# Two of four weight sums per column pair: from VectorE subtractions to transfers that add in SBUF

## The chip, the cores and the metric

The kernel runs on one core of one Trainium2 chip. The metric is device time of one execution in microseconds (us). Every instruction and transfer of one profiled execution is in the trace. PE is TensorE's matmul row, PEld its weight loads, DVE is VectorE, ACT is ScalarE, POOL is GpSimd, SP is SyncE, which only issues transfers. A PE product can wait for DVE, which can wait for ACT, which waits for transfers; the text speaks of such chains by these names.

## The reference

One layer of a streaming encoder for 512 prompt tokens and 32 sample tokens (544 together), width 1024. What matters here is the first large product, the input projection, whose columns then feed three branches:

```python
h = rmsnorm(x, g1)
z = h @ w_in
(mq, mk, mv, mo, mi, mf, sb, sc, sx, dq, dk, dv, gt) = jnp.split(z, splits, axis=-1)
...
proj = jnp.einsum('btnc,ncd->btnd', br, w_br)
gates = jax.nn.sigmoid(gt.reshape(Bsz, T, N_BRANCH, D_MODEL))
x = x + jnp.einsum('btnd,btnd->btd', gates, proj) @ w_o
h2 = rmsnorm(x, g2)
up = h2 @ w_up
...
x = x + (jax.nn.silu(upc[..., :D_FF]) * upc[..., D_FF:]) @ w_dn
```

The three branches are an mLSTM recurrence (`ml` steps), a short convolution, and differential attention (`at` steps); everything is float32.

## The kernel before, in words

**Products.** Float32 accuracy is made of three reduced-precision matmuls: weight and activation are each split into a high and a low part (`w_h`, `w_l`, `a_h`, `a_l`), and high times high, low times high and high times low are summed in PSUM. All weights stream from HBM. A weight goes through: a transfer by SP into one of four slots of `raw` (512 KB each, `NRAW`), a copy by ACT that rounds to `w_h` (L1033), a subtraction by DVE that leaves `w_l` (L1332), then the matmuls. The parts have five slots (`NSPLIT`). One slot holds a unit of four 128x128 weight tiles; DVE and ACT split a unit four units (`AHEAD`) before PE multiplies with it.

**Pairs.** Thirty groups of 256 columns of `w_in` are called pairs: ("mq", 0), ("mv", 0), ..., ("sx", 1), ..., ("gt2", 3). A pair's weight is a 2x2 block matrix: two halves of the 1024 rows by two blocks of 128 columns, B11, B12, B21, B22, each 128 partitions x 512 floats (256 KB). The activations are 2x2 too (row half by token half). Each pair is computed with seven block products instead of eight, numbered w = 1 to 7 and run by `strassen_product`, twelve matmuls of 272 columns each. Products 1, 2 and 3 take a block of weights straight from `raw` (B11, B21, B22); products 4 to 7 take sums T4 to T7 of blocks. DVE makes these in `make_t` into four places of the buffer `tw`: T7 = B22 - B12, T5 = B12 - B11, T6 = T7 + B11, T4 = B21 - T6. Where the two items of a pair lie in neighbouring slots of `raw` (29 of the 30 pairs, `both`), T7 and T5 are one instruction of 1024 floats a partition (L1352); else each sum is one of 512 (L1356). The left factors S1 to S4 are sums of activations, made once at the start.

**Order.** All engines walk one list, `ORDER`, of products, drains, `ml`, `at` and `post` steps; each engine takes its own steps from it, in order, and waits on semaphores. `T_MAKES` says at which unit DVE makes a sum: T6 and T4 two units before they are split (`u_of(q, 6) - AHEAD - 2`), T7 and T5 a unit earlier. SP loads a pair's two items ((q, 0) with B11 and B12, (q, 1) with B21 and B22) in the order of use; a slot of `raw` is loaded again when its last reader is through (`wait_item_read`). POOL takes small steps of the `ml` and `at` chains (L840 to L842, L889, L951, L952), output transfers, and the low parts L929 and L846.

After the pairs come the output projection, the up-projection with its convolution, and the down-projection, which the change does not touch.

Of the kernel before, what the change touches and what calls it, by code (L numbers as in the profile page):

```python
# [6 lines left out]
ALU = mybir.AluOpType  # L7
# [3 lines left out]
P = 128  # L11
DM = 1024
# [38 lines left out]
def streaming_encoder_step(nc, x_prompt, x_sample, cache_k, cache_v, state_C, state_n, state_m, state_conv,  # L51
# [306 lines left out]
    def u_of(pair, w):  # L358
        return first_unit[n_of(pair, w)]


    both = [q for q in pairs if ITEMS.index((q, 0)) % NRAW + 1 == ITEMS.index((q, 1)) % NRAW]
    for q in pairs:
        u6 = u_of(q, 6) - AHEAD
        for w, e in ((7, u6 - 3), (6, u6 - 2), (5, u6 - 3 if q in both else u_of(q, 5) - AHEAD - 2),
                     (4, u_of(q, 4) - AHEAD - 2)):
            T_MAKES.setdefault(e, []).append((q, w))
    assert min(T_MAKES) >= 0
    for e in sorted(T_MAKES):
        for x in T_MAKES[e]:  # L370
            t_no[x] = len(t_no)
    for q, q2 in zip(pairs, pairs[1:]):
        made = {x: e for e, xs in T_MAKES.items() for x in xs}
        for w in T_SLOT:
            assert made[(q2, w)] > u_of(q, w) - AHEAD, (q, w)
        assert t_no[(q2, 6)] > t_no[(q, 4)] > t_no[(q, 6)] > t_no[(q, 7)]

# [48 lines left out]
    with ctx:  # L426
# [155 lines left out]
        for nm in (  # L582
# [4 lines left out]

                "wh_ready wl_ready t_ready part_used "

# [85 lines left out]

        def scale_of(pair):
            return 64 ** -0.5 if pair[0] == "dq" else 1.0

# [21 lines left out]
        def t_view(pair, w):  # L700
            return tw[:, T_SLOT[w], :].rearrange("p (k f) -> p k f", k=KQ)

# [11 lines left out]
        def wait_item(eng, item):  # L714
            i = ITEMS.index(item)
            eng.wait_ge(raw_in[i % NRAW], 16 * (i // NRAW + 1))

        def wait_whole(eng, g):

            what, w = UNITS[g][0:2]  # L720
            if g == 0:
                eng.wait_ge(S["if_in"], 16)
            elif what not in pair_no:
                wait_item(eng, what)
            elif w in QUARTER:
                wait_item(eng, (what, QUARTER[w][0]))
            else:
                eng.wait_ge(S["t_ready"], t_no[(what, w)] + 1)

# [28 lines left out]
        def _(sp):  # L758
# [18 lines left out]
            for i, item in enumerate(ITEMS):  # L777
# [35 lines left out]
        def _(pool):  # L813
# [179 lines left out]
        def _(act):  # L993
# [56 lines left out]
            for kind, a, n in ORDER:  # L1050
# [87 lines left out]
                elif kind == "p" and a[1] in copied[a[0]]:  # L1138
# [14 lines left out]
                    if w == 1 and q == ("sc", 0):  # L1153
                        act.wait_ge(S["dense_done"], block_of[("pr", 0, KD - 1)] + 1)
                    sc.activation(dst_of(q, blk, half), chain_bank(q, w), ACT.Copy, scale=scale_of(q))\
                        .then_inc(S["act_drained"], 1)
# [154 lines left out]
        def _(dve):  # L1311
# [23 lines left out]
            def make_t(q, w):  # L1335

                i = pair_no[q]
                B11, B12, B21, B22 = (quarter(q, k, blk) for k in range(2) for blk in range(2))
                x, y, op = {7: (B22, B12, ALU.subtract), 6: (t_view(q, 7), B11, ALU.add), 5: (B12, B11, ALU.subtract),
                            4: (B21, t_view(q, 6), ALU.subtract)}[w]  # L1340
# [4 lines left out]
                if w in (6, 4):  # L1345
                    dve.wait_ge(S["t_ready"], t_no[(q, {6: 7, 4: 6}[w])] + 1)
                if q in both and w == 7:
                    if i:
                        dve.wait_ge(S["wl_ready"], u_of(pairs[i - 1], 5) + 1)
                    s0 = ITEMS.index((q, 0)) % NRAW  # L1350
                    b = raw[:, s0:s0 + 2, :].rearrange("p s (k f) -> p s k f", k=KQ)
                    v.tensor_tensor(tw[:, 0:3:2, :].rearrange("p s (k f) -> p s k f", k=KQ), b[:, :, :, P:2 * P],  # L1352
                                    raw[:, s0, :].rearrange("p (k s f) -> p s k f", k=KQ, s=2), ALU.subtract)\
                        .then_inc(S["t_ready"], 2)
                elif not (q in both and w == 5):
                    v.tensor_tensor(t_view(q, w), x, y, op).then_inc(S["t_ready"], 1)  # L1356

# [20 lines left out]
            for kind, a, n in ORDER:  # L1378
# [57 lines left out]
                elif kind == "left":  # L1436
                    F11, F21 = (f_x[:, 0:KQ, HALF * half:HALF * half + HALF] for half in range(2))
                    F12, F22 = (f_x[:, KQ:KD, HALF * half:HALF * half + HALF] for half in range(2))
                    if a[0] == 0:
                        dve.wait_ge(S["f_ready"], KD)  # L1440
                        sum_left(a_f[:, S1], F21, F22, ALU.add)
                        dve.wait_ge(S["s_ready"], 1)
                        sum_left(a_f[:, S2], a_f[:, S1], F11, ALU.subtract)
                        sum_left(a_f[:, S3], F11, F21, ALU.subtract)
                    elif a[0] == 1:
                        dve.wait_ge(S["s_ready"], 3)
                        dve.wait_ge(S["al_ready"], KD)
                        sum_left(F11, F12, a_f[:, S2], ALU.subtract)
# [679 lines left out]
```

## Time and profile before

| | |
|---|---|
| median of 3 runs | 993.11 us (991.67 to 993.19) |
| profiled execution, its own time | 993.04 us |
| span of its instructions | 991.2 us |
| PE busy | 971.5 us (98%) |
| DVE busy | 690.3 us (70%) |
| ACT busy | 472.4 us (48%) |
| POOL busy | 162.8 us (16%) |
| SP's transfer queue, share of 16 DMA engines | 28.2% |

The span runs from the first to the last instruction; 1.8 us of the execution lie outside it. The pairs occupy PE from about 49 us to 518 us. A matmul of 272 columns starts 0.126 us after the one before it, so a product of twelve takes 1.51 us; the trace shows each as some 0.29 us long, because they overlap.

### The profile page before, as it was taken

The page shows a single profiled execution, that of the slowest core. Times are in us where ns is not written, and L with a number is a line of the kernel's source. Part 1 is how long each engine was busy: PE and PEld are TensorE (multiplying, and loading weights), DVE is VectorE, ACT ScalarE, POOL GpSimd, SP SyncE. Part 2 cuts the span into 40 slices and gives each one's busy share as a digit, 9 for nine tenths or more (in the row PEclk, how much of TensorE's full clock was granted, in tenths as well). Part 3 has the DMA queues.
Part 4 walks back from the last instruction along what each step waited for, and adds up shares of the span by engine and source line. Part 5 has one row for each costly group of instructions (what it writes and reads, how often), then busy time and mean ns, then how long its engine had stood idle before and what let it go on. Part 6 is the DMA issues. An engine that isn't in the chain of part 4 may idle for free.

```text
span 991.2 us, 20106 instructions
## 1 busy us (share of the span) xinstructions
PE 971.5 (98%) x7749; PEld 949.6 (96%) x7749; DVE 690.3 (70%) x1161; ACT 472.4 (48%) x982; POOL 162.8 (16%) x346
## 2 busy tenths in 40 slices
PE   7999999999999999999999999999999999999996
PEld 6999899998999998999999999999999999999996
DVE  7887666688666899877775547777777777634354
ACT  5675455565565766555553333333333333322242
POOL 2000121110111222021112211111111111111011
PEclk9999999999999999999999999999999999999999
DMA  6522323264321223233244212222222222432252
GB/s 198 197 86 86 93 92 108 68 197 136 104 85 45 86 86 86 64 89 105 66 134 168 86 61 92 85 97 91 89 86 87 85 86 81 128 94 76 84 148 94
DMA packets 104086, 99.87 MB, mean 101 GB/s; under 512 B 4868, under 2 KB 99481, under 8 KB 103735
## 3 DMA queue, kind: packets, MB, share of 16 engines
q1 hardware_dynamic: 98799, 85.51, 28.2%
q10 hardware_dynamic: 4072, 10.23, 3.0%
q0 software_dynamic: 1120, 2.86, 0.8%
q8 instruction: 62, 1.02, 0.4%
q14 instruction: 33, 0.27, 0.1%
HBM read 91.26 MB, written 7.31 MB: 99 GB/s over the span
## 4 chain that ended last, share of the span: by engine, by line
PE 90%; DVE 4%; issue 2%; ACT 2%; DMA 0%; POOL 0%; DVEq 0%; POOLq 0%; ACTq 0%
PE D L1751 51%; PE D L1810 28%; PE D L1770 2%; PE X L2045 1%; PE X L2083 1%; DVE w_l L1332 1%; ACT w_h L1033 1%; PE D L1782 1%; PE D L1937 1%; PE D L1895 1%; PE X L1991 1%; PE X L1992 0%; PE X L1977 0%; DVE tw L1352 0%; PE X L1994 0%
## 5 line engine op out<-in xcount | busy, mean ns | idle before, releaser
L1332 DVE TENSOR_TENSOR w_l<-raw,w_h 128x512 fp32r<-128x512 f32 (+1 forms) x286 | 201.0, 720 | 131.2 <-ACT w_h L1033 128.9
L1810 PE MATMUL D<-a_h,w_h 128*128 128x272 f32 x840 | 250.4, 298 | 1.4 <-DVE tmp L1513 1.0
L1810 PE MATMUL D<-a_h,w_l 128*128 128x272 f32 x840 | 243.6, 290 | 0.0
L1810 PE MATMUL D<-a_l,w_h 128*128 128x272 f32 x840 | 242.3, 288 | 0.0
L1033 ACT ACTIVATE w_h<-raw 128x512 fp32r<-128x512 f32 (+1 forms) x286 | 171.5, 617 | 82.8 <-PE D L1751 71.7
L1810 PEld LDWEIGHTS D<-a_h,w_h 128*128 128x128 f32 x840 | 158.7, 189 | 5.6 <-issue 2.6
L1810 PEld LDWEIGHTS D<-a_l,w_h 128*128 128x128 f32 x840 | 159.1, 189 | 0.0
L1810 PEld LDWEIGHTS D<-a_h,w_l 128*128 128x128 f32 x840 | 158.6, 189 | 0.0
L1751 PE MATMUL D<-h_h,w_h 128*128 128x272 f32 x704 | 145.9, 288 | 0.1
L1751 PE MATMUL D<-h_h,w_l 128*128 128x272 f32 x704 | 145.7, 288 | 0.0
L1751 PE MATMUL D<-h_l,w_h 128*128 128x272 f32 x704 | 145.1, 288 | 0.0
L1332 DVE TENSOR_TENSOR w_l<-tw,w_h 128x512 fp32r<-128x512 f32 x120 | 83.7, 704 | 39.6 <-ACT w_h L1033 33.6
L1751 PEld LDWEIGHTS D<-h_h,w_h 128*128 128x128 f32 x704 | 110.6, 188 | 0.3 <-DVE ups L1703 0.3
L1292 ACT ACTIVATE acc<-ups,fcw 128x546 f32<-128x546 f32 x44 | 33.1, 753 | 162.7 <-POOL ffn_last L975 162.7
L1751 PEld LDWEIGHTS D<-h_l,w_h 128*128 128x128 f32 x704 | 110.6, 188 | 0.0
L1751 PEld LDWEIGHTS D<-h_h,w_l 128*128 128x128 f32 x704 | 109.9, 189 | 0.0
L1033 ACT ACTIVATE w_h<-tw 128x512 fp32r<-128x512 f32 x120 | 75.2, 631 | 42.5 <-PE D L1751 15.0
L1751 PE MATMUL D<-g_h,w_h 128*128 128x272 f32 x352 | 80.6, 290 | 0.0
L1751 PE MATMUL D<-g_l,w_h 128*128 128x272 f32 x352 | 79.8, 288 | 0.0
L1751 PE MATMUL D<-g_h,w_l 128*128 128x272 f32 x352 | 79.8, 288 | 0.0
L1706 DVE SCALAR_TENSOR_TENSOR acc<-ups,fcw,acc 128x546 f32<-128x546 f32 x44 | 34.7, 789 | 57.9 <-ACT acc L1292 57.9
L1751 PEld LDWEIGHTS D<-g_h,w_h 128*128 128x128 f32 x352 | 57.9, 188 | 0.3 <-DVE xT L1682 0.2
(359 smaller groups left out, 1670.2 us busy)
## 6 DMA issues: line engine op xcount, KB each, us to landing
raw<-in_w_in SPq DMA_DIRECT2D x64, 512.0 KB, 4.2
raw<-in_w_up SPq DMA_DIRECT2D x44, 512.0 KB, 4.1
raw<-in_w_down SPq DMA_DIRECT2D x20, 512.0 KB, 3.8
raw<-in_w_branch SPq DMA_DIRECT2D x12, 512.0 KB, 3.4
raw<-in_w_out SPq DMA_DIRECT2D x8, 512.0 KB, 4.4
raw<-in_w_down SPq DMA_DIRECT2D x10, 384.0 KB, 3.5
x_spill<-xT ACTq DMA_DIRECT2D x1, 2176.0 KB, 7.4
xT<-x_spill ACTq DMA_DIRECT2D x1, 2176.0 KB, 10.3
```

The source lines that it names most:

```text
L1033: sc.activation(split_view(w_h, g), whole_view(g), ACT.Copy).then_inc(S["wh_ready"], 1)
L1292: sc.activation(acc[part][:, j % 2, 0:T + 2], ups[m % 2][:, 2:T + 4], ACT.Copy, scale=fcw[:, 2, jj:jj + 1])\
L1332: v.tensor_tensor(split_view(w_l, g), whole_view(g), split_view(w_h, g).bitcast(F32), ALU.subtract)\
L1706: link(v.scalar_tensor_tensor(out=ac, in0=u[:, 1:T + 3], scalar=fcw[:, 1, jj:jj + 1], in1=ac, op0=ALU.mult, op1=ALU.add))
L1751: last = t.matmul(banks(n)[:, half if at_bank is None else at_bank, 0:HALF], w[:, k, :], x[:, kx + k, HALF * half:HALF * half + HALF], sta ...
L1770: last = t.matmul(banks(n)[0:w.shape[2], half, 0:HALF], w[:, k, :], left_of(x, kx)[:, half, :], start=kx == 0 and i == 0, stop=kx == KD - ...
L1782: last = t.matmul(banks(n)[0:w.shape[2], half, 0:HALF], w[:, k, :], left_of(x, kx)[:, half, :], start=kx == 0 and i == 0, stop=kx == KD - ...
L1810: last = t.matmul(out, wt[:, k, :], x[:, left, k, :], start=w in (1, 2, 5) and k == i == 0, stop=k == KQ - 1 and i == 2, skip_group_check= ...
L1895: last = t.transpose(B[:, j // 4, P * (j % 4):P * (j % 4) + L], src[:, P * j:P * j + P], ident[0:L, 0:L])
L1937: last = t.transpose(B[:, P * c:P * c + P], src_tok(name, j)[:, P * c:P * c + P], ident[:])
L1991: t.matmul(o, qi[:, h, 0:L], C[:, h, :], start=True, stop=False)
L2045: t.matmul(X[:, c, 0:nk], dqT[d, h, P * i:P * i + P], dkT[d, h, 0:nk], start=True, stop=False, skip_group_check=True)
```

## The change

T5 and T7 are no longer made by DVE. For each pair:

- T7 = B12 + B22 is formed in place: POOL issues a transfer (`accum_op=add`) that reads B22 from HBM again and adds it to B12 where that lies in `raw`. Product 7 then takes its weight from `raw`.
- T5 = B11 + B12: SP loads B11 a second time, into place 0 or 2 of `tw` (alternating from pair to pair), and POOL issues a second adding transfer that brings B12.
- POOL issues both at a place of `ORDER` six units before the pair's first product (`SUMS_AT`), after waiting for the loads that they add to.
- DVE still makes T6 = T7 + B11 and T4 = B21 + T6, and now waits for the T7 transfer before T6; ACT waits for the T5 transfer before it splits T5.
- Since the sums are additions now, S1, S2 and S4 change sign, and the results of column block 1 are drained with scale -1.
- The slot of item (q, 0) is free only when T7 has been split, not when DVE has made T5, T6 and T7.

```diff
-T_SLOT = {5: 0, 6: 1, 7: 2, 4: 3}
+T_SLOT = {6: 1, 4: 3}
...
+    SUMS_AT = {}
     for q in pairs:
-        u6 = u_of(q, 6) - AHEAD
-        for w, e in ((7, u6 - 3), (6, u6 - 2), (5, u6 - 3 if q in both else u_of(q, 5) - AHEAD - 2),
-                     (4, u_of(q, 4) - AHEAD - 2)):
+        for w, e in ((6, u_of(q, 6) - AHEAD - 2), (4, u_of(q, 4) - AHEAD - 2)):
             T_MAKES.setdefault(e, []).append((q, w))
+        SUMS_AT.setdefault(max(u_of(q, 1) - 6, 1), []).append(q)
...
         def t_view(pair, w):
-            return tw[:, T_SLOT[w], :].rearrange("p (k f) -> p k f", k=KQ)
+            if w == 7:
+                return quarter(pair, 0, 1)
+            slot = 2 * (pair_no[pair] % 2) if w == 5 else T_SLOT[w]
+            return tw[:, slot, :].rearrange("p (k f) -> p k f", k=KQ)
...
-                eng.wait_ge(S["wl_ready"], max(u_of(q, w) for w in ((1,), (2, 3))[k]) + 1)
-                eng.wait_ge(S["t_ready"], max(t_no[(q, w)] for w in ((5, 6, 7), (4, 7))[k]) + 1)
+                eng.wait_ge(S["wl_ready"], max(u_of(q, w) for w in ((1, 7), (2, 3))[k]) + 1)
+                eng.wait_ge(S["t_ready"], t_no[(q, (6, 4)[k])] + 1)
...
+                if kind in pair_no and item[1] == 0:
+                    q = item[0]
+                    if pair_no[q] >= 2:
+                        sp.wait_ge(S["wl_ready"], u_of(pairs[pair_no[q] - 2], 5) + 1)
+                    sp.dma_start(t_view(q, 5), weight_quarter(q, 0, 0)).then_inc(S[f"t5_in{pair_no[q] % 2}"], 16)
...
+            def weight_sums(q):
+
+                wait_item(pool, (q, 0))
+                g.dma_start(t_view(q, 7), weight_quarter(q, 1, 1), accum_op=ALU.add).then_inc(S[f"t7_ready{pair_no[q] % 2}"], 16)
+                pool.wait_ge(S[f"t5_in{pair_no[q] % 2}"], 16 * (pair_no[q] // 2 + 1))
+                g.dma_start(t_view(q, 5), weight_quarter(q, 0, 1), accum_op=ALU.add).then_inc(S[f"t5_ready{pair_no[q] % 2}"], 16)
...
-                for k in {7: (0, 1), 6: (0,), 5: (0,), 4: (1,)}[w]:
-                    wait_item(dve, (q, k))
+                if w == 6:
+                    dve.wait_ge(S[f"t7_ready{i % 2}"], 16 * (i // 2 + 1))
+                    if i:
+                        dve.wait_ge(S["t_ready"], t_no[(pairs[i - 1], 4)] + 1)
+                    x, y = t_view(q, 7), quarter(q, 0, 0)
+                else:
+                    wait_item(dve, (q, 1))
+                    dve.wait_ge(S["t_ready"], t_no[(q, 6)] + 1)
+                    x, y = quarter(q, 1, 0), t_view(q, 6)
...
-                        sum_left(a_f[:, S1], F21, F22, ALU.add)
+                        sum_left(a_f[:, S1], F22, F21, ALU.subtract)
                         dve.wait_ge(S["s_ready"], 1)
-                        sum_left(a_f[:, S2], a_f[:, S1], F11, ALU.subtract)
+                        negative_left(a_f[:, S2], a_f[:, S1], F11)
```

How the rows move is shown at the pair ("sx", 1), whose T6 the prediction comes back to. On DVE, round the place where its sums are made (`tw` holds sums, `raw` the loaded weights, `w_l` the low parts; `u_c` belongs to the short convolution), before:

```order
L1332 TENSOR_TENSOR w_l<-raw,w_h 128x512
L1356 TENSOR_TENSOR tw<-raw,tw 128x512
L1352 TENSOR_TENSOR tw<-raw 128x2x512
L1633 MEMSET u_c 128x2
L1635 TENSOR_TENSOR u_c<-tmp,scb 128x2x240
L1635 TENSOR_TENSOR u_c<-tmp,scb 128x2x32
L1641 COPY u_c<-vec 128x2
L1332 TENSOR_TENSOR w_l<-raw,w_h 128x512
L1356 TENSOR_TENSOR tw<-tw,raw 128x512
```

and now:

```order
L1376 TENSOR_TENSOR tw<-raw,tw 128x512
L1658 MEMSET u_c 128x2
L1660 TENSOR_TENSOR u_c<-tmp,scb 128x2x240
L1660 TENSOR_TENSOR u_c<-tmp,scb 128x2x32
L1666 COPY u_c<-vec 128x2
L1359 TENSOR_TENSOR w_l<-raw,w_h 128x512
L1376 TENSOR_TENSOR tw<-raw 128x512
```

The instruction of 2 x 512 is gone; T4 of the pair before and T6 of this one stand where they stood, with nothing else moved. On POOL, at the same pair (`assq` and `arr` are steps of an attention norm, `conv_last` of the convolution):

```order
L857 TENSOR_TENSOR assq<-assq,m_half 128x1
L858 TENSOR_TENSOR arr<-assq,rsum 128x1
L873 DMA raw<-in_w_in 128x4x128
L875 DMA tw<-in_w_in 128x4x128
L950 COPY conv_last<-u_c 128x2
L951 COPY conv_last<-u_c 128x2
```

The two adding transfers are new; before, the copy to `conv_last` came right behind the step that writes `arr`.

## Rows read from the trace of the kernel before

**Rows 1.** First part of the page: busy time by engine.

```profile
PE 971.5 (98%) x7749; PEld 949.6 (96%) x7749; DVE 690.3 (70%) x1161; ACT 472.4 (48%) x982; POOL 162.8 (16%) x346
```

**Rows 2.** Busy time in stretches: the pairs, and 354 to 399 us.

```profile
core 0: us, PE busy (x) PEld busy (x) DVE busy (x) ACT busy (x) POOL busy (x), PEclk, DMA share, GB/s
45.00:524.00 479.00, 473.68 (x3803) 456.25 (x3803) 357.65 (x628) 278.81 (x651) 75.54 (x138) 1.00 0.32 98
354.00:399.00 45.00, 41.78 (x322) 39.31 (x321) 40.29 (x79) 28.18 (x72) 8.35 (x19) 1.00 0.25 71
```

**Rows 3.** Waits of PE, 45 to 524 us: total, times, longest.

```profile
PE X L2066 <- DVE prob L1375: 1.2, 2, 0.7
PE X L2089 <- ACT wdT L1267: 1.0, 1, 1.0
PE D L1810 <- DVE tmp L1513: 1.0, 1, 1.0
PE X L2001 <- DVE qi L1588: 0.8, 1, 0.8
PE D L1946 <- DVE f_tmp L1513: 0.6, 1, 0.6
```

**Rows 4.** Instructions on the tile tw: min/median/max ns, first and last start.

```profile
L1352 DVE TENSOR_TENSOR tw<-raw x29: 1206/1218/1222, 41.5 to 495.3; 128x1024 f32<-128x1024 f32 x29
```

**Rows 5.** Chain that ended last, 179 to 190 us: start, length.

```profile
181.83 1.14 DVE tw L1352
...
185.47 0.69 DVE qi L1588
```

**Rows 6.** The same chain, 350 to 400 us.

```profile
358.59 1.22 DVE tw L1352
...
372.10 1.21 DVE tw L1352
...
389.07 1.13 DVE tw L1352
```

**Rows 7.** Order of time round ("sx", 1), per engine: start, length, instruction.

```profile
317.38 0.95 DVE L1332 TENSOR_TENSOR w_l<-tw,w_h 128x512 fp32r<-128x512 f32 x1
...
311.62 0.92 SPq L795 DMA_DIRECT2D raw<-in_w_in  x2
...
329.84 0.62 ACT L1033 ACTIVATE w_h<-raw 128x512 fp32r<-128x512 f32 x1
...
329.63 0.24 POOL L842 TENSOR_TENSOR arr<-assq,rsum 128x1 f32<-128x1 f32 x1
...
334.49 0.68 DVE L1356 TENSOR_TENSOR tw<-tw,raw 128x512 f32<-128x512 f32 x1
...
338.08 0.68 DVE L1332 TENSOR_TENSOR w_l<-tw,w_h 128x512 fp32r<-128x512 f32 x1
...
342.31 0.29 PE L1810 MATMUL D<-a_h,w_h 128*128 128x272 f32 x1
```

**Rows 8.** Transfers by line: count, size of each, us from issue to landing.

```profile
raw<-in_w_in SPq DMA_DIRECT2D x64, 512.0 KB, 4.2
...
out<-C_p POOLq DMA_DIRECT2D x1, 256.0 KB, 3.6
...
out<-C_p POOLq DMA_DIRECT2D x1, 2.0 KB, 8.1
```

**Rows 9.** Order of time round 206 us, POOL and DVE.

```profile
205.95 0.84 POOL L899 DMA_DIRECT2D out<-C_p  x1
...
206.58 0.68 DVE L1332 TENSOR_TENSOR w_l<-raw,w_h 128x512 fp32r<-128x512 f32 x1
```

**Rows 10.** Order of time round ("gt1", 1) and ("gt2", 3), POOL and DVE.

```profile
384.79 0.19 POOL L842 TENSOR_TENSOR arr<-assq,rsum 128x1 f32<-128x1 f32 x1
...
391.08 0.68 DVE L1356 TENSOR_TENSOR tw<-tw,raw 128x512 f32<-128x512 f32 x1
...
490.51 1.37 POOL L929 TENSOR_TENSOR mg_l<-merged,mg_h 128x544 fp32r<-128x544 f32 x1 [4.76 <-ACT mg_h L1173]
...
497.39 0.68 DVE L1356 TENSOR_TENSOR tw<-tw,raw 128x512 f32<-128x512 f32 x1
```

More of the change, by code:

```diff
@@ L375, in streaming_encoder_step @@
             assert made[(q2, w)] > u_of(q, w) - AHEAD, (q, w)
-        assert t_no[(q2, 6)] > t_no[(q, 4)] > t_no[(q, 6)] > t_no[(q, 7)]
+        assert t_no[(q2, 6)] > t_no[(q, 4)] > t_no[(q, 6)]
     tmp_row, tmp_before, holder = {}, {}, [None] * 6
@@ L586, in streaming_encoder_step @@
                 "dense_done act_drained dve_drained "
-                "wh_ready wl_ready t_ready part_used "
+                "wh_ready wl_ready t_ready t5_in0 t5_in1 t5_ready0 t5_ready1 t7_ready0 t7_ready1 part_used "
                 "f_ready s_ready ah_ready al_ready "
@@ L674, in dst_of, with scale_of @@
             return tmp_pair(pair)[:, blk, cols]
-        def scale_of(pair):
-            return 64 ** -0.5 if pair[0] == "dq" else 1.0
+        def scale_of(pair, blk):
+            return (64 ** -0.5 if pair[0] == "dq" else 1.0) * (-1.0 if blk else 1.0)
         def two(ap):
@@ L700, in t_view, with weight_quarter @@
         def t_view(pair, w):
-            return tw[:, T_SLOT[w], :].rearrange("p (k f) -> p k f", k=KQ)
+            if w == 7:
+                return quarter(pair, 0, 1)
+            slot = 2 * (pair_no[pair] % 2) if w == 5 else T_SLOT[w]
+            return tw[:, slot, :].rearrange("p (k f) -> p k f", k=KQ)
+        def weight_quarter(pair, k, blk):
+            name, jj = pair
+            at_col = (BRANCH_AT + DM * int(name[2]) if name[:2] == "gt" else W_IN_AT[name]) + 2 * P * jj + P * blk
+            return w_in[0][BW * k:BW * k + BW, at_col:at_col + P].rearrange("(k p) f -> p k f", p=P)
         def whole_view(g):
@@ L726, in wait_whole @@
                 wait_item(eng, (what, QUARTER[w][0]))
+            elif w in T_SLOT:
+                eng.wait_ge(S["t_ready"], t_no[(what, w)] + 1)
             else:
-                eng.wait_ge(S["t_ready"], t_no[(what, w)] + 1)
+                eng.wait_ge(S[f"t{w}_ready{pair_no[what] % 2}"], 16 * (pair_no[what] // 2 + 1))
         def wait_split_slot(eng, g):
@@ L852, in _ @@
             g.memset(gates_l[:, :, H:32].bitcast(F32), 0.0).then_inc(S["gates_zeroed"], 1)
+            def weight_sums(q):
[3 more added lines that the diff above has]
+                g.dma_start(t_view(q, 5), weight_quarter(q, 0, 1), accum_op=ALU.add).then_inc(S[f"t5_ready{pair_no[q] % 2}"], 16)
             for kind, a, n in ORDER:
+                if n is not None:
+                    for u in units(n):
+                        for q in SUMS_AT.get(u, []):
+                            weight_sums(q)
                 if kind == "xT":
@@ L1154, in _ @@
                         act.wait_ge(S["dense_done"], block_of[("pr", 0, KD - 1)] + 1)
-                    sc.activation(dst_of(q, blk, half), chain_bank(q, w), ACT.Copy, scale=scale_of(q))\
+                    sc.activation(dst_of(q, blk, half), chain_bank(q, w), ACT.Copy, scale=scale_of(q, blk))\
                         .then_inc(S["act_drained"], 1)
@@ L1337, in make_t @@
                 i = pair_no[q]
-                B11, B12, B21, B22 = (quarter(q, k, blk) for k in range(2) for blk in range(2))
-                x, y, op = {7: (B22, B12, ALU.subtract), 6: (t_view(q, 7), B11, ALU.add), 5: (B12, B11, ALU.subtract),
-                            4: (B21, t_view(q, 6), ALU.subtract)}[w]
-                for k in {7: (0, 1), 6: (0,), 5: (0,), 4: (1,)}[w]:
-                    wait_item(dve, (q, k))
+                if w == 6:
[7 more added lines that the diff above has]
+                    x, y = quarter(q, 1, 0), t_view(q, 6)
                 if i:
                     dve.wait_ge(S["wl_ready"], u_of(pairs[i - 1], w) + 1)
[L1345 to L1356, printed above, removed]
+                v.tensor_tensor(t_view(q, w), x, y, ALU.add).then_inc(S["t_ready"], 1)
             def low_left(q):
@@ L1364, in sum_left, with negative_left @@
                 v.tensor_tensor(out, x, y, op).then_inc(S["s_ready"], 1)
+            def negative_left(out, x, y):
+                v.scalar_tensor_tensor(out=out, in0=x, scalar=-1.0, in1=y, op0=ALU.mult, op1=ALU.subtract)\
+                    .then_inc(S["s_ready"], 1)
             def combine(u, p0, p1):
@@ L1447, in _ @@
                         dve.wait_ge(S["al_ready"], KD)
-                        sum_left(F11, F12, a_f[:, S2], ALU.subtract)
+                        negative_left(F11, F12, a_f[:, S2])
                         low_left(S1)
@@ L1511, in _ @@
                     wait_drained(dve, n_of(q, {2: 1, 3: 6}.get(w, 12 - held[q])))
-                    out, src = dst_of(q, *{2: (0, 0), 3: (1, 0)}.get(w, (1, 1))), chain_bank(q, w if w in (2, 3) else held[q])
-                    v.scalar_tensor_tensor(out=out, in0=src, scalar=scale_of(q), in1=out, op0=ALU.mult, op1=ALU.add)\
+                    blk, half = {2: (0, 0), 3: (1, 0)}.get(w, (1, 1))
+                    out, src = dst_of(q, blk, half), chain_bank(q, w if w in (2, 3) else held[q])
+                    v.scalar_tensor_tensor(out=out, in0=src, scalar=scale_of(q, blk), in1=out, op0=ALU.mult, op1=ALU.add)\
                         .then_inc(S["dve_drained"], 1)
```

1 line of the change is left out of this document (removed).

## The prediction

> **What bounds the kernel now.** I read the busy times first, then the stretches, then PE's waits, then the chain that ended last. PE is busy for 971.5 of 991.2 us and DVE for 690.3 [rows 1], so over the whole kernel work taken from DVE buys nothing unless PE waits for it. All that the change touches lies in the stretch of the pairs, 45 to 524 us. There PE is busy for 473.68 of 479.00 us [rows 2]: 5.3 us of idle time is all that can be won there without changing PE's own work. The five largest waits make 4.6 us of it, and four of these rows name DVE [rows 3]; the fifth, 1.0 us for ACT's `wdT`, stands in a stretch where ACT itself queues behind DVE. The idle time is not spread out: 45.00 - 41.78 = 3.2 us of it falls between 354 and 399 us, where DVE is busy for 40.29 of 45 us, 90%, against 75% over all pairs [rows 2]. There, and only there, DVE is nearly the bound. The chain shows the same from the other side: in front of PE's stalls it runs through DVE, with the combined T7-and-T5 instruction L1352 in it at 358.59, 372.10 and 389.07 us [rows 6], and at 181.83 us ahead of the `qi` for which PE then waits 0.8 us [rows 3, 5].
>
> Everywhere else DVE is ahead of PE. At the pair ("sx", 1) `w_l` of T6 is done at 338.08 + 0.68 = 338.76 us and PE starts that product at 342.31 [rows 7]: a lead of 3.5 us. I compared the end of `w_l` with PE's start in the same way for all the products of the pairs: the lead is between 1.2 and 10.8 us. It matters twice below: it is why most of the freed DVE time buys nothing, and it is the cover over the new waits.
>
> **What goes.** The change removes 29 combined instructions at 1.218 us [rows 4] and for the thirtieth pair two of half that size: 30 x 1.22 = 37 us of DVE. Almost all of it lies beside a busy PE and is worth nothing. Worth something are the waits above:
> - 354 to 399 us, 3.2 us of idle PE: three instructions of 1.2 us leave this stretch and two more leave the 25 us ahead of it, while DVE has only 45 - 40.3 = 4.7 us of slack in it. DVE falls to (40.3 - 3.7)/45 = 81%, so I let the waits there go but for 0.2 us: 3.0 us.
> - 185 us: `qi` is reached through DVE work that includes L1352 3.6 us before it. It comes up to 1.1 us sooner, which covers the wait of 0.8: 0.8 us.
> - The 0.6 us for `f_tmp` has T6 ahead of it, which stays; DVE is only earlier by what it has saved before. I count a third: 0.2 us.
>
> Together 4.0 us.
>
> **What is added.** T6 and T4 stay as they were; the turned signs change a constant in instructions that are there anyway. Nothing moves on PE or ACT. Three things are new.
>
> *The two adding transfers.* No row shows a transfer that adds. Nearest is the store of `C_p`, issued by POOL too and of the same shape, 128 partitions by four runs of 512 bytes: 0.84 us of POOL to issue [rows 9] and 3.6 us from issue to landing [rows 8]. An adding one reads its target as well, so 3.6 us is the lower bound. The upper one is the slowest row of POOL's queue, 8.1 us for a store of 4-byte pieces [rows 8]. I take about 4.5, nearer to the row of equal shape. Is it in time? POOL comes to the pair ("sx", 1) when its `arr` is done, 329.63 + 0.24 = 329.87 us; with 3.6 us T7 lies there at 333.5. DVE comes to T6 at 334.49 [rows 7], and without L1352 1.2 us earlier, 333.3: just met. At ("gt2", 3): 490.51 + 1.37 + 3.6 = 495.5 against 497.39; at ("gt1", 1): 384.79 + 0.19 + 3.6 = 388.6 against 391.08 [rows 10]. These are the three tightest of the thirty, with 1.0, 1.9 and 2.5 us to spare against the old times; all others have 3.5 us or more, 7.7 on average. A late T6 holds back DVE, and PE only when the lead is eaten: at ("sx", 1) 8.1 us would make T6 late by 8.1 - 3.6 - 1.0 = 3.5 us, just the lead of 3.5. So at either bound the transfers cost PE nothing, but at the upper one five or six pairs give DVE's relief back, at most 1.5 us of the 4.0. T5 is split later than T6 is made in most pairs, or at nearly the same time; its transfer follows 0.84 us behind, and has at least 1.5 us to spare.
>
> The Trainium skill has a rule against this ("SBUF — State Buffer", Who interferes with whom): descriptors of POOL's transfers are written through a port that DVE locks in its two-port modes, and the page has such a transfer go from 0.62 to 3.1 us. By it each would land some 2.5 us later, an estimate from that page, and the sum would be nearer to -3.5 than to -4.0 us. The trace shows no such starving: the issue of `C_p` took 0.84 us beside subtractions that took their ordinary 0.68 [rows 9].
>
> *POOL's time.* Two issues of 0.84 us in each pair, 50 us in all, on an engine that is busy for 75.5 of 479 us [rows 2]. Behind them queue `conv_last`, the norm steps and the copies of `yc`. POOL waited several us for ACT or DVE ahead of nearly each of these, so they start no later. I count nothing; if that cover were gone, 1.7 us a pair would reach ACT and, after the lead, PE.
>
> *The slot of (q, 0).* It is held until `w_l` of T7. For ("sx", 1) the slot comes free at 317.38 + 0.95 = 318.3 us; its load was issued at about 312 before. With 4.2 us it lands at 322.5, and ACT's first use of it is at 329.84 [rows 7, 8]: 7 us of cover. SP's new wait, for T5 of the pair before last, is over before the slot is free, so nothing queues longer. The load of B11 and the two additions bring 30 x 3 x 256 KB = 23.6 MB over the 479 us, 49 GB/s more than the 98 there, at a DMA share of 0.32 [rows 2]; I count nothing.
>
> **Sum.** 993.0 of the profiled execution - 3.0 - 0.8 - 0.2 = 989.0 us. That execution stands at the median of the runs (993.11), so this is the forecast for the median too. All 5.3 us and a little start-up after each wait, which the idle time leaves out, would make 987.
>
> **Rivals.**
> - *The relief does not reach PE.* The waits in 354 to 399 us hang on a ping-pong of DVE, ACT and PE in attention, and ACT may take DVE's place in it; ACT is at 28.18 of 45 us there [rows 2], which speaks against. The gain would be 0 to 2 us: 991 to 993.
> - *Slow additions,* the case on the other side. If one takes 12 us from issue to landing, T6 at ("sx", 1) is 12 - 3.6 - 1.0 = 7.4 us late and PE stands for 7.4 - 3.5 = 3.9 us. The same reckoning for all thirty pairs gives 17 late ones and 11 us of standing; with most of the relief lost, about 1002 us. It decides near 10 us: there the pairs cost 3 us and the relief is used up. Nothing in the rows is that slow, but none of them adds.
> - *More than the idle time.* If PE's 5.3 us understate what it loses, DVE's 37 us could be worth more: PEld is idle for 479.00 - 456.25 = 22.7 us [rows 2], so at most 993.0 - 22.7 = 970 us. The Trainium skill ("Perfetto Trace Analysis", Identifying the Most-Contended Engine) says that headroom on TensorE is read from the weight loads, not from matmul time. Against it: most of that idle time is at small products of attention and mLSTM, whose matmuls outlast their loads.
>
> **How the numbers follow.** Transfers in time and the stalls gone: 0.62, 987 to 991, 989.0 the likeliest. Relief that does not reach PE: 0.18, 991 to 993.5. Slow additions: 0.17, of which 0.05 within 2 us of before and 0.12 above. More than the idle time: 0.03. What a measurement of this kernel can tell from no change is about 0.2%, 2 us. Faster: 0.62 + 0.03 = 0.65; same: 0.18 + 0.05 = 0.23; slower 0.12. The range reaches from the whole idle time won, 987, to additions of about 10 us, 996.
>
> **What would show it.** Right: no L1352, T6 starting with no wait or one under 1 us; PE's idle time from 45 to 524 us at 1 to 2 us; adding transfers landing in 3.6 to 8 us; DVE's share in 354 to 399 us near 80%. Wrong: rows in which DVE waits for `raw` ahead of T6, or ACT for `tw` ahead of `w_h`, for several us in many pairs, and PE behind them; POOL issues far over 0.84 us; slower loads into `raw`.

## The result and the profile after

The changed kernel takes 994.75 us, the median of 15 runs (993.17 to 998.09), against 991.87 us for the kernel before on the same chip: ratio 1.0026 [1.002, 1.0033], slower by 2.9 us between the medians where 4.0 us faster was forecast. The profiled execution took 993.89 us, with a span of 991.9. The 15 executions of the kernel before fall into two groups some 1.3 us apart, ten of 991.47 to 992.22 and five of 992.86 to 993.19, and the profiled one, 993.04, is of the longer group: its trace has a stretch at the lower clock, shown in the last section.

First the busy times by engine on the page of after, as [rows 1]:

```profile
PE 971.3 (98%) x7749; PEld 948.9 (96%) x7749; DVE 659.3 (66%) x1130; ACT 471.5 (48%) x982; POOL 240.1 (24%) x406
```

The stretches of [rows 2] in the trace after:

```profile
45.00:524.00 479.00, 472.69 (x3800) 454.56 (x3799) 327.29 (x596) 276.68 (x650) 149.62 (x195) 1.00 0.67 145
354.00:399.00 45.00, 43.42 (x336) 40.99 (x335) 37.66 (x77) 28.88 (x74) 19.66 (x28) 1.00 0.64 127
```

The change did what it says: DVE lost 31 us, where the prediction counted 37, and in the stretch from 354 to 399 us PE stands for 1.6 us where it stood for 3.2. Yet over all pairs PE now stands for 479.00 - 472.69 = 6.3 us in place of 5.3. So other waits have come. PE's waits in the pairs (total, times, longest) against [rows 3]:

```profile
PE X L2091 <- DVE prob L1399: 3.4, 3, 1.8
PE D L1835 <- ACT tmp L1182: 0.6, 1, 0.6
PE D L1835 <- DVE tmp L1538: 0.5, 1, 0.5
PE D L1776 <- issue: 0.5, 1, 0.5
...
PE X L2026 <- DVE qi L1613: 0.3, 1, 0.3
```

The wait for `wdT` is gone as forecast, that for `f_tmp` is gone too, of which only a third was counted on, and that for `qi` is down from 0.8 to 0.3, where all of it was to go. But `prob` takes 3.4 us where it took 1.2. Who holds DVE, ACT and POOL is read from their own waits for transfers, which no row of before had for these tiles:

```profile
DVE tw L1376 <- DMA raw<-in_w_in: 7.1, 3, 3.1
...
ACT w_h L1060 <- DMA tw<-in_w_in: 5.7, 3, 4.6
...
POOL raw L873 <- DMA raw<-in_w_in: 71.2, 12, 12.4
```

L1376 is T6, waiting for the addition that makes T7 in `raw`: late in 3 of the 30 pairs. ACT's `w_h` waits for T5 three times. POOL's own wait is for the load of (q, 0), on which it adds.

The place with the dearest wait is ("sx", 1), [rows 7]. In order of time, SP, POOL, DVE, ACT and PE (start, length, instruction, idle time before it and its releaser):

```profile
317.98 0.37 SPq L806 DMA_DIRECT2D raw<-in_w_in  x1
...
329.25 0.24 POOL L858 TENSOR_TENSOR arr<-assq,rsum 128x1 f32<-128x1 f32 x1
329.57 1.35 POOL L873 DMA_DIRECT2D raw<-in_w_in  x1
330.43 1.82 POOL L875 DMA_DIRECT2D tw<-in_w_in  x1
...
336.17 0.69 DVE L1376 TENSOR_TENSOR tw<-raw 128x512 f32<-128x512 f32 x1 [3.10 <-DMA raw<-in_w_in]
...
338.64 1.22 DVE L1628 TENSOR_REDUCE nmax<-X 128x2 f32<-128x1024 f32 x1
339.77 0.68 DVE L1359 TENSOR_TENSOR w_l<-tw,w_h 128x512 fp32r<-128x512 f32 x1
...
340.01 0.68 ACT L1283 ACTIVATE prob<-X,nmax 128x512 f32<-128x512 f32 x1
...
345.17 0.75 DVE L1399 SCALAR_TENSOR_TENSOR prob<-prob,kap 128x512 f32<-128x512 f32 x1
...
345.97 0.44 PE L2091 MATMUL X<-ident,prob 128*128 128x128 f32 x2 [1.83 <-DVE prob L1399]
```

Read it downwards. The load that POOL adds on was issued at 318.0 and landed 3.7 us later, at 321.7. POOL issues the addition only at 329.57, right behind its own `arr`. It releases T6 at 336.17, 6.6 us after the issue, and DVE has stood for 3.10 us. Behind T6 in DVE's order stand `nmax`, the `w_l` of T6 (339.77) and, some steps later, `prob`: 338.64 us for `nmax` and 345.17 for `prob`, where the trace before has them at 336.95 and 343.13. PE waits 1.83 us for `prob`. In the trace before, DVE and PE stand so at this `prob`:

```profile
343.13 0.75 DVE L1375 SCALAR_TENSOR_TENSOR prob<-prob,kap 128x512 f32<-128x512 f32 x1
...
343.94 0.33 PE L2066 MATMUL X<-ident,prob 128*128 128x128 f32 x1
```

PE waited for nothing there, but DVE was done at 343.13 + 0.75 = 343.88 us, so the lead was only 0.06 us.

POOL's queue as a whole on the page of after (packets, MB, share of 16 engines):

```profile
q0 software_dynamic: 32800, 18.59, 14.3%
```

The two additions by their lines, first T7's, then T5's (min/median/max ns of the issue, and us from issue to landing):

```profile
L873 POOL DMA_DIRECT2D raw<-in_w_in x30: 1265/1344/1530, 34.7 to 492.2; - x30
...
DMA to landing us min/median/max: 4.6/4.7/11.1
...
L875 POOL DMA_DIRECT2D tw<-in_w_in x30: 1280/1822/1886, 35.7 to 493.0; - x30
...
DMA to landing us min/median/max: 4.5/6.0/13.5
```

### The profile page after: what moved, and what is told of

The parts are those of the page before. It is cut to its first block, busy times and chain, and to the rows that moved or that the text cites. A ratio compares the mean times of both kernels' runs of the same rounds, so it can differ in the third digit from the quotient of the medians.

```text
span 991.9 us, 20076 instructions
## 1 busy us (share of the span) xinstructions
PE 971.3 (98%) x7749; PEld 948.9 (96%) x7749; DVE 659.3 (66%) x1130; ACT 471.5 (48%) x982; POOL 240.1 (24%) x406
## 3 DMA queue, kind: packets, MB, share of 16 engines
q0 software_dynamic: 32800, 18.59, 14.3%
## 4 chain that ended last, share of the span: by engine, by line
PE 58%; issue 1%; DVE 1%; DMA 1%; ACT 1%; POOL 0%; POOLq 0%; ACTq 0%; DVEq 0%
PE D L1776 48%; PE D L1835 7%; DMA raw<-in_w_in 1%; PE X L1884 0%; PE X L2108 0%; PE X L1776 0%; PE X L2070 0%; DVE nmax L1628 0%; PE X L1850 0%; DVE w_l L1359 0%; PE X L2091 0%; PE X L1857 0%; ACT yst L1161 0%; ACT prob L1283 0%; POOL yc_l L979 0%
## 5 line engine op out<-in xcount | busy, mean ns | idle before, releaser
L1359 DVE TENSOR_TENSOR w_l<-raw,w_h 128x512 fp32r<-128x512 f32 (+1 forms) x316 | 221.8, 719 | 140.5 <-ACT w_h L1060 137.9
L1060 ACT ACTIVATE w_h<-raw 128x512 fp32r<-128x512 f32 (+1 forms) x316 | 190.2, 618 | 91.8 <-PE D L1776 76.3
L1359 DVE TENSOR_TENSOR w_l<-tw,w_h 128x512 fp32r<-128x512 f32 x90 | 63.2, 708 | 43.2 <-ACT w_h L1060 37.1
L1060 ACT ACTIVATE w_h<-tw 128x512 fp32r<-128x512 f32 x90 | 56.8, 631 | 35.3 <-PE D L1835 9.8
L873 POOL DMA_DIRECT2D raw<-in_w_in x30 | 40.0, 1334 | 94.4 <-DMA raw<-in_w_in 94.0
```

The source lines that it names most:

```text
L873: g.dma_start(t_view(q, 7), weight_quarter(q, 1, 1), accum_op=ALU.add).then_inc(S[f"t7_ready{pair_no[q] % 2}"], 16)
L1060: sc.activation(split_view(w_h, g), whole_view(g), ACT.Copy).then_inc(S["wh_ready"], 1)
L1359: v.tensor_tensor(split_view(w_l, g), whole_view(g), split_view(w_h, g).bitcast(F32), ALU.subtract)\
```

## The experiments

Three theories stood at the start. **L**: DVE's relief is real, and the sums that come too late eat it. **T**: the transfers' traffic and POOL's issues cost by themselves. **N**: the relief never reaches PE.

**1. The relief alone** (e1_relief). Products 5 and 7 take bare quarters, and nothing is transferred for them.

```diff
-            if w == 7:
-                return quarter(pair, 0, 1)
+            if w in (5, 7):
+                return quarter(pair, 0, w // 7)
...
-                    dve.wait_ge(S[f"t7_ready{i % 2}"], 16 * (i // 2 + 1))
+                    wait_item(dve, (q, 0))
```

> Leaves out: the sums of products 5 and 7, which take the bare quarters B11 and B12; no load of B11 into tw and no adding transfer is issued, the rest is the changed kernel. It shows what the freed DVE time alone is worth. Before is 991.9. Theory L (the sums come too late, and DVE and ACT stand for them): the relief is real, 988 to 990, ratio 0.996 to 0.998, as the prediction's 4.0 us had it. Theory T (the transfers' traffic and POOL's issues cost by themselves): the same, 988 to 990. Theory N (the relief never reaches PE): 991 to 992.5.

987.63 us against 992.39, ratio 0.9951 [0.9938, 0.9965], a little below what L and T expected. The stretch of the pairs in this run:

```profile
45.00:524.00 479.00, 477.27 (x3852) 460.78 (x3852) 332.89 (x602) 279.65 (x654) 75.69 (x139) 1.00 0.35 102
```

All of PE's waits in it:

```profile
PE X L2083 <- DVE prob L1391: 0.7, 1, 0.7
PE D L1827 <- ACT mqT L1174: 0.4, 1, 0.4
PE X L2018 <- DVE qi L1605: 0.3, 1, 0.3
PE X L2008 <- DVE p_ml L1582: 0.3, 1, 0.3
```

The relief is worth 4.8 us between the medians. N has fallen.

**2. The traffic, with nobody waiting** (e2_traffic). As 1, but all 30 loads and 60 additions are issued, onto two places of `tw` that nobody reads (the same parts of the products are left out).

```diff
-                g.dma_start(t_view(q, 7), weight_quarter(q, 1, 1), accum_op=ALU.add)
+                g.dma_start(high, weight_quarter(q, 1, 1), accum_op=ALU.add)
...
-                g.dma_start(t_view(q, 5), weight_quarter(q, 0, 1), accum_op=ALU.add)
+                g.dma_start(low, weight_quarter(q, 0, 1), accum_op=ALU.add)
```

> As e1_relief, but the load of B11 and both adding transfers of each pair are issued at the same places of SP's and POOL's programs, into places that nobody reads; DVE and ACT wait for none of them. Theory L: within 1 us of e1_relief (988 to 991). Theory T: 3 to 5 us above e1_relief, at the changed kernel's 994 to 995. Theory N: 991 to 993, and e1_relief there too.

988.79 us, ratio 0.9955 [0.9942, 0.9967]. The median is 1.2 us above that of 1, a little more than the 1 us that L allowed but within its 988 to 991; the intervals overlap, and the profiled executions have spans of 985.6 and 985.5 us. A DMA share of 0.68 in place of 0.35 and twice the time of POOL (152.35 us) cost PE nothing that these two traces show. T has fallen; what costs is the waiting.

**3. All sums by DVE in the changed kernel** (e3_dve), two additions of 512 floats, T7 in place in `raw`:

```diff
+                if w == 5:
...
+                    v.tensor_tensor(t_view(q, 5), quarter(q, 0, 0), quarter(q, 0, 1), ALU.add).then_inc(S["t_ready"], 1)
...
+                if w == 7:
...
+                    v.tensor_tensor(t_view(q, 7), t_view(q, 7), quarter(q, 1, 1), ALU.add).then_inc(S["t_ready"], 1)
```

> The changed kernel with its turned signs, places and order, but with DVE forming all sums of 5 and 7 (two additions of about 0.68 us in a pair, one event ahead of T6) and no transfer. All theories: within 1.5 us of before (991 to 993), ratio 0.999 to 1.0015; if it is at 994 or more, the signs or the order cost, and none of the theories holds.

994.48 us, ratio 1.002 [1.0011, 1.0028]: outside the expectation, and by its own words against all three theories, had not experiment 8 cleared the signs and experiment 1 the order. PE's waits:

```profile
PE X L2122 <- DVE prob L1430: 1.8, 3, 0.8
PE X L2145 <- ACT wdT L1309: 1.3, 1, 1.3
PE D L1866 <- DVE tmp L1569: 1.3, 1, 1.3
PE X L2057 <- DVE qi L1644: 1.1, 1, 1.1
PE D L2002 <- DVE f_tmp L1569: 0.9, 1, 0.9
```

These are the waits of [rows 3], each 0.3 us longer but for the first of the two for `prob`, which is as it was, and a new one of 0.2 for another `prob`. Two instructions of 0.68 us take 0.14 us more than one of 1.22 [rows 4]; that these waits grow by about two such steps fits, but was not tested apart.

**4. Plain loads in place of the additions** (e4_plain), with the same waits and bytes (products 5 and 7 then use B12 and B22):

```diff
-                g.dma_start(t_view(q, 7), weight_quarter(q, 1, 1), accum_op=ALU.add)
+                g.dma_start(t_view(q, 7), weight_quarter(q, 1, 1))
...
-                g.dma_start(t_view(q, 5), weight_quarter(q, 0, 1), accum_op=ALU.add)
+                g.dma_start(t_view(q, 5), weight_quarter(q, 0, 1))
```

> The changed kernel with POOL's two transfers as plain loads over the same places, with the same waits (products 5 and 7 use B12 and B22 in place of the sums). It prices the addition. Theory L with the addition itself as what is slow: POOL's issue falls to about 0.9 us, landing to about 3.6 to 4.2 us, 990 to 992. Theory L with the way to the queue as what is slow (POOL's late issue behind raw, other traffic): landing stays at 4.5 to 6 us and the time at 993.5 to 995. Theory T: 993 to 995, since bytes and issues are the same. Theory N: 992 to 995.

988.47 us, ratio 0.9959 [0.9946, 0.9971], faster than any theory had it; issue and landing fall as L has it with the addition itself as what is slow. POOL's queue on the page of this run, to be held against the changed kernel's above:

```profile
q0 software_dynamic: 5920, 18.59, 6.4%
```

The two loads by their lines:

```profile
L873 POOL DMA_DIRECT2D raw<-in_w_in x30: 749/833/991, 34.5 to 488.8; - x30
...
DMA to landing us min/median/max: 3.2/3.5/8.2
...
L875 POOL DMA_DIRECT2D tw<-in_w_in x30: 749/749/782, 35.5 to 489.6; - x30
...
DMA to landing us min/median/max: 3.3/3.7/9.0
```

The same bytes without the addition land in 3.5 and 3.7 us instead of 4.7 and 6.0, and POOL's issue takes 0.83 and 0.75 us (medians) instead of 1.34 and 1.82. One T6 still waits, 1.4 us. So at the price of a plain transfer, near the prediction's lower bound of 3.6 us, the forecast would have come true.

**5. POOL's order** (e5_order). The next runs ask whether the price of the addition decides, or the place of its issue.

```diff
+    LEAD = {12: 9, 17: 7, 19: 7, 20: 8, 23: 7, 29: 9}
...
-        SUMS_AT.setdefault(max(u_of(q, 1) - 6, 1), []).append(q)
+        SUMS_AT.setdefault(max(u_of(q, 1) - LEAD.get(pair_no[q], 6), 1), []).append(q)
```

> The changed kernel with POOL's two issues moved 1 to 3 units up in its program for 6 of the 30 pairs (numbers 12, 17, 19, 20, 23, 29), where POOL came to them only after its own arr or mg_l though the raw load had landed 5 to 9 us before. Theory L-order (late because POOL is late at the issue): PE's waits at 340.86, 345.97 and 502.25 us (0.27, 1.83, 0.49 us, and 0.29 us of start-up each) go, 3.5 us: 990 to 991.5, ratio 0.998 to 1.000. Theory L-price (late because an addition lands in 5 to 13 us, wherever it is issued, or POOL now stands for raw and holds arr and yc back): 993 to 996.

993.77 us, ratio 1.0013 [1.0004, 1.0022]: by the number this is L-price's range. But all the waits named there are gone, and that at 398 us too; a new one ate the gain. POOL, DVE and PE round 208 us in this run:

```profile
204.72 1.28 POOL L876 DMA_DIRECT2D tw<-in_w_in  x1 [3.69 <-DMA tw<-in_w_in]
...
207.46 0.20 POOL L859 TENSOR_TENSOR rr<-ssq,rden 128x4 f32<-128x4 f32 x1
...
207.69 0.69 DVE L1614 TENSOR_TENSOR qi<-X,rr 128x512 f32<-128x512 f32 x1 [3.68 <-POOL rr L859]
...
208.53 0.85 PE L2027 MATMUL X<-ident,qi 128*128 128x128 f32 x4 [3.51 <-DVE qi L1614]
```

This is pair number 12, the one place where the move was wrong: POOL stands 3.69 us for the load into `tw`, and its `rr`, now behind that wait, is late for `qi`.

**6. The same, with pair 13 left to DVE** (e6_order13), with the instructions of experiment 3.

```diff
+    BY_DVE = {7: {13}, 5: {13}}
```

> As e5_order, and DVE forms both sums of pair number 13, ('gt0', 1), whose raw load landed only at 220.5 us and whose additions took 11 and 13 us. Theory L-order: the waits at 234.84 and 241.75 us (0.51 and 0.59 us and the start-up of each) go too, 1.7 us below e5_order: 988.5 to 990, ratio 0.996 to 0.998. Theory L-price: within 1 us of e5_order, at 993 or more.

993.41 us, ratio 1.001 [1.0001, 1.0019]: within 1 us of experiment 5, again as L-price had it, because the wait at 208 us is there too (3.27 us); the waits near 235 to 246 us are gone.

**7. T5 alone by transfer** (e7_t5only), T7 as in experiment 3.

```diff
+    BY_DVE = {7: set(range(30)), 5: set()}
```

> T5 alone by transfer, as in the changed kernel; DVE forms T7 in place (0.68 us in each pair), so T6 waits for no transfer. Half of DVE's relief is left, 30 x 0.54 = 16 us. If late T7 is what costs (T6 and the attention steps behind it): PE's wait of 1.83 us is gone, 990 to 992. If late T5 costs (ACT standing at w_h): 993 to 995.

989.75 us, ratio 0.9975 [0.9965, 0.9985], just below the range given for late T7. Some 2.4 us faster than before, with half the relief. No engine waits for a sum; `wdT` and `tmp` keep 0.5 and 0.4 us of their old 1.0 each.

**8. The signs alone** (e8_signs), in the kernel before.

```diff
-                x, y, op = {7: (B22, B12, ALU.subtract), 6: (t_view(q, 7), B11, ALU.add), 5: (B12, B11, ALU.subtract),
-                            4: (B21, t_view(q, 6), ALU.subtract)}[w]
+                x, y, op = {7: (B22, B12, ALU.add), 6: (t_view(q, 7), B11, ALU.add), 5: (B12, B11, ALU.add),
+                            4: (B21, t_view(q, 6), ALU.add)}[w]
...
-                    sc.activation(dst_of(q, blk, half), chain_bank(q, w), ACT.Copy, scale=scale_of(q))\
+                    sc.activation(dst_of(q, blk, half), chain_bank(q, w), ACT.Copy, scale=scale_of(q, blk))\
```

> The kernel before with the turned signs alone: the sums stay on DVE in the combined instruction, as additions. If the signs cost nothing and the 2.1 us of e3_dve are its two instructions in place of one: within 0.7 us of before, ratio 0.9993 to 1.0007. If the signs or the constants cost: 993.5 to 994.5, as e3_dve.

991.84 us, ratio 0.9998 [0.9989, 1.0007]. The signs cost nothing.

**9. POOL's order without pair 12** (e9_order5).

```diff
-    LEAD = {12: 9, 17: 7, 19: 7, 20: 8, 23: 7, 29: 9}
+    LEAD = {17: 7, 19: 7, 20: 8, 23: 7, 29: 9}
```

> As e5_order without pair number 12, whose issue stays where the changed kernel has it. In e5_order POOL stood there for raw and tw with rr behind it, and PE waited 3.51 us for qi at 208.53 us. Theory L-order: that wait goes and no other comes, 3.8 us below e5_order: 989.5 to 991, ratio 0.997 to 0.999. Rival (the additions cost wherever they are put, and one wait only gives way to the next): 992 to 994.

991.14 us, ratio 0.9986 [0.9977, 0.9995], just above L-order's range and below the rival's: the wait for `qi` at 208 us is gone. Pair 13, ("gt0", 1), is what is left: T6 stood 4.32 us there in the profiled execution, and PE 2.5 us behind it.

**10. The same, with pair 13 left to DVE** (e10_order5_13).

```diff
+    LEAD = {17: 7, 19: 7, 20: 8, 23: 7, 29: 9}
+    BY_DVE = {7: {13}, 5: {13}}
```

> As e9_order5, with both sums of pair number 13 formed by DVE. Theory L-order: the waits near 235 to 246 us go too: 988 to 990, ratio 0.996 to 0.998, within 1.5 us of e1_relief's 987.6, where nothing waits for a sum. Rival: 992 to 994.

987.55 us (987.36 to 987.79), ratio 0.9947 [0.9935, 0.996]: 4.8 us faster than before, some 7 us faster than the changed kernel, and as fast as experiment 1, which had no sums to wait for; L-order had 988 to 990. The stretch of the pairs in this run:

```profile
45.00:524.00 479.00, 477.27 (x3851) 460.70 (x3850) 334.10 (x604) 279.58 (x654) 150.50 (x195) 1.00 0.68 148
```

PE's waits in it (two more of 0.3 us are left out):

```profile
PE X L2123 <- DVE prob L1431: 0.7, 1, 0.7
PE D L1867 <- ACT mqT L1198: 0.4, 1, 0.4
```

POOL's issue and DVE's T6 at ("sx", 1), in order of time:

```profile
320.73 1.36 POOL L886 DMA_DIRECT2D raw<-in_w_in  x1 [3.41 <-DMA raw<-in_w_in]
...
331.33 0.68 DVE L1408 TENSOR_TENSOR tw<-raw 128x512 f32<-128x512 f32 x1
```

PE is busy for the same 477.27 us as in experiment 1, with the medians of the additions as they were (4.7 and 6.1 us): T7 is now issued 10.6 us before T6 takes it, not 6.6, and neither DVE nor ACT waits for a transfer of weights anywhere in the pairs. At the moved places the additions landed sooner as well: T7 at ("sx", 1) in 4.9 us instead of 6.6, T5 at ("gt1", 1) in 5.7 instead of 8.5 and at ("gt2", 3) in 5.6 instead of 8.2. So the move changed when an addition starts and how long it takes; no run parts the two.

**11. T7 by transfer in four pairs only** (e11_mixed).

```diff
-    BY_DVE = {7: {13}, 5: {13}}
+    BY_DVE = {7: set(range(30)) - {21, 22, 23, 24}, 5: {13}}
```

> As e10_order5_13, but T7 by transfer only in pairs number 21 to 24, around the stretch from 354 to 399 us where DVE is nearly the bound; DVE forms T7 everywhere else, and T5 comes by transfer in all pairs but number 13. Theory L-order: DVE's time outside that stretch is worth nothing, so 988 to 990, within 1 us of e10_order5_13. Rival (DVE's relief counts all over): 1 to 3 us above e10_order5_13.

988.48 us, ratio 0.9957 [0.9945, 0.9969], with the same four waits of PE as in 10: outside the stretch from 354 to 399 us DVE's time for T7 is worth nothing that can be told.

**12. T7 alone by transfer** (e12_t7only).

```diff
+    BY_DVE = {7: set(), 5: set(range(30))}
...
+                if w == 5:
...
+                    v.tensor_tensor(t_view(q, 5), t_view(q, 6), quarter(q, 1, 1), ALU.subtract).then_inc(S["t_ready"], 1)
```

> The mirror of e7_t5only: T7 alone by transfer, and DVE forms T5 as T6 less B22, right behind T6 (0.68 us in each pair, and all of it behind the wait for T7). POOL issues where the changed kernel does. If late T7 is what costs: the waits at 340 to 346 us stay, 993 to 996. If T5's transfer was the costly one: 990 to 991.5.

996.15 us, ratio 1.0037 [1.0023, 1.0051], just above the range given for late T7, and the waits near 341 and 346 us stay. PE waits 3.1 us for `prob`, and 1.1 for `qi` and `p_ml` each. DVE stands for a transfer twice, 3.5 us in all. Some of this is late T7, some that DVE does more behind T6; the run does not part them.

## Why the prediction was wrong

**What bounds the kernel, and what the relief is worth: right.** 4.0 us was forecast. Experiment 1 measured 4.8 between the medians, with an interval of some 3.5 to 6. Where it comes from is seen by holding the start of the same product in the two traces against each other: the trace before falls back by 0.65 us at 90 us (`f_tmp`), 0.47 at 186 (`qi`), 1.11 at 366 (`wdT`), 1.13 at 380 (`tmp`) and 0.77 at 398 (`prob`), 4.1 us at the very places that the prediction named. Their idle time is 3.6; the rest is the start-up that the prediction had left out, 0.1 us a stall. (The 0.29 us that some expectations counted for it is a matmul's own length, and too much.) The total came out better than its terms. For the stretch from 354 to 399 us 3.0 was forecast, and so it was, although one wait of 0.7 for `prob` stays there, because the start-ups made up for it. But `qi` gave 0.47 instead of 0.8, and `f_tmp` 0.65 instead of 0.2: two misses that cancel by luck. Another 1.5 us by which the two spans differ is no relief: it is a stretch at the lower clock, shown at the end. It is also in the 993.0 us from which the forecast was counted; from the median of 15 executions, 991.87, the same sum gives 987.9. "More than the idle time" goes no further: the weight loads, which by the Trainium skill ("Perfetto Trace Analysis", Identifying the Most-Contended Engine) are one of two measures of the headroom, are still idle for 479.00 - 460.78 = 18.2 us in experiment 1, and no run came near them.

**The price of the additions: too low, but within its bounds for most.** About 4.5 us was taken; the medians are 4.7 for T7 and 6.0 for T5. T7 broke the upper bound of 8.1 in pair 13 alone, with 11.1 us, and T5 in six pairs: 13.5 us in pair 13 and 8.2 to 8.5 in pairs 12, 16, 23, 26 and 29. In pair 13 a plain transfer (experiment 4) is slow too, 8.2 and 9.0 us. The four dearest T7 (pairs 13, 16, 19 and 23, 6.5 to 11.1 us) stand beside loads that SP issued within 1.5 us of them, but others beside such loads took 4.6 to 5.6; whether the loads are the reason was not tested.

**"So at either bound the transfers cost PE nothing": this step failed.** It let a late T6 reach PE only through T6's own `w_l`, which leads by 3.5 us. That lead held: at ("sx", 1) T6 started 336.17 - 334.49 = 1.7 us later than before [rows 7], its `w_l` was done at 339.77 + 0.68 = 340.45 us, PE took it at 342.47, and no product waited for it. But DVE works in order, and what stands behind T6 has no such lead: `prob` had 0.06 us. There it is the drain `scb`, for which PE stood 0.27 us, and above all `nmax` and `prob`, 1.7 and 2.0 us late, and PE stood 1.83 us for `prob`. In pair 13 it is the drain `tmp`, in pair 23, ("gt1", 1), `prob` again.

The other half of the step is T5. "At either bound" was reckoned for T6 alone; T5 was given at least 1.5 us to spare, and no sum is shown for it at 8.1 us. In pair 29 POOL issued it at 492.97 us, it took 8.2 us, and ACT, which had taken T5 at 498.48 in the trace before, stood 4.58 us for it until 501.23; PE's wait of 0.49 us at 502.25, for which the profile names no releaser, is gone where this addition is issued earlier (experiments 5 and 10).

The six waits that the changed kernel has and experiment 10 has not are 0.51, 0.59, 0.27, 1.83, 0.91 and 0.49 us, 4.6 in all. By the starts of the same products the changed kernel falls back by 0.67, 0.70, 0.43, 2.05, 1.13 and 0.65 us at these six places, 5.6 of the 991.9 - 985.7 = 6.2 by which the spans differ. So four pairs of thirty cost more than the whole relief, 5.6 us against 4.1 in the profiled executions. Three of them are those that the prediction had named as the tightest, ("sx", 1), ("gt1", 1) and ("gt2", 3). The medians differ by more, 2.9 us: the changed kernel's profiled execution lies 0.9 us below its median, its 15 executions spread over 4.9 us against 1.7 before, and what the longer ones have more no trace shows.

**POOL's time "counted at nothing": right for the traffic, wrong for its order.** The traffic rose by 47 GB/s, from 98 to 145, where 49 were reckoned. The issues took 1.34 and 1.82 us, not 0.84, and cost nothing where POOL had time (experiment 2). But where POOL came to the addition only after `arr` or `mg_l`, its place in the order set the landing: moved up by one to three units in five pairs, with pair 13 left to DVE, it costs nothing any more (experiments 9 and 10). The prediction counted these issues behind `arr` correctly and took the place as given; it asked whether POOL's later steps start late, not how long the loaded quarter lies ready before POOL comes: 7.8 us at ("sx", 1). The wrong move in experiment 5 shows the price of the other side, 3.5 us, when POOL waits with a needed step behind it.

**The rivals.** "Slow additions" named the right mechanism and the wrong threshold: it had the loss begin near 10 us for all pairs, since it counted only the lead of `w_l`. It began below 6.6 us, the price of T7 at ("sx", 1), and the three tightest pairs and number 13 were enough. "The relief does not reach PE" fell with experiment 1.

**The rule of the port** (the Trainium skill, "SBUF — State Buffer", Who interferes with whom: DVE's two-port modes lock out the writing of POOL's descriptors): the prediction put it at 2.5 us for each transfer, more than the section gives. It says that `tensor_tensor`, most of DVE's work beside these issues, has no two-port mode. Were such a lock what lengthens the issues, it would have lengthened the plain ones of experiment 4 as well, which stand at the same places. They took 0.83 and 0.75 us. So the longer issue belongs to the addition; no run here shows the lock.

**The slot of (q, 0) and the signs:** the signs cost nothing (experiment 8). The slot by itself costs nothing either: experiment 1 holds it until T7's `w_l` as well. But the prediction looked at ("sx", 1) alone. In pair 13 the load of (q, 0) was issued at 206.86 us instead of 200.01 and landed at 220.53 instead of 208.92, POOL stood 12.4 us for it, and only then could the slow addition start. No run parts the later load from the slow addition there.

## What to carry to other kernels

When an instruction is made to wait for a transfer, ask of everything queued behind it on its engine how much lead that has; the lead of its own consumer covers only that one. Work moved off a busy engine is worth its waits and their start-ups, and it must be issued when its input is ready: look for the in-order step ahead of the issue, and leave the few places where neither engine has spare time as they were. One run without the moved work and one with the work that nobody waits for tell relief, traffic and waiting apart.

## What the hardware showed that was not expected

- A transfer that adds is cut finer than a plain one of the same shape. Without the 1120 packets that the queue has in experiment 1, 60 additions make (32800 - 1120)/60 = 528 packets each and 60 plain loads (5920 - 1120)/60 = 80, for the same 18.59 MB. Engine time, less the 0.9% of experiment 1: (14.3 - 0.9)% of 16 engines against (6.4 - 0.9)%, 2.4 times as much. The Trainium skill ("Collectives: The Full Stack", The bandwidth ceiling: the fold count and why AG ≠ RS ≠ AR) says for ring collectives that the add needs two source reads, so that a reduce-scatter moves at half the rate of an all-gather, which copies; the 2.4 is not far from that, in a transfer that is no collective. The finer cut may have its part in the 2.4, and no run parts the two.
- An addition holds POOL longer as well: 1.34 us for the first and 1.82 for the one behind it, against 0.83 and 0.75.
- A DMA share of 0.68 in place of 0.35 over 479 us left the time of a kernel that is bound by PE where it was (experiments 1, 2 and 10).
- In its profiled execution the kernel before had a stretch at the lower clock of 1.2 GHz in which PE was never idle, and experiment 1 had none. The rows of both, and of experiment 4, whose profiled execution had such a stretch at the same place (columns as in [rows 2]; the granted clock is the third from the end), before:

```profile
110.00:114.00 4.00, 4.00 (x28) 2.20 (x26) 3.06 (x4) 0.92 (x2) 0.00 (x0) 1.00 0.02 4
114.00:117.00 3.00, 3.00 (x15) 2.89 (x13) 0.47 (x3) 0.00 (x0) 0.00 (x0) 0.50 0.00 0
```

experiment 1:

```profile
110.00:114.00 4.00, 4.00 (x27) 2.13 (x26) 1.78 (x3) 0.92 (x2) 0.00 (x0) 1.00 0.49 135
114.00:117.00 3.00, 3.00 (x24) 3.00 (x25) 0.68 (x4) 1.26 (x5) 0.00 (x0) 1.00 0.00 0
```

experiment 4:

```profile
114.00:117.00 3.00, 3.00 (x16) 2.92 (x15) 0.46 (x3) 0.21 (x1) 0.00 (x0) 0.60 0.26 78
```

  Ahead of it PE was busy throughout, with matmuls that outlast their loads (2.20 of 4 us of weight loads), but so it was in experiment 1 (2.13 of 4). By the starts of the same matmuls the stretch cost PE 1.5 us. Why the clock fell in some executions and not in others was not followed up.
